# Two mixture-of-experts layers: experts sorted by their tokens, packed into 128-row sets in strips of 32

## The reference

```python
scores = sigmoid(h @ w_router)                       # n_tok x 64
_, idx = top_k(scores + e_bias, 8)                   # 8 experts for each token
wts = take(scores, idx); wts = wts / wts.sum() * 2.5
for e in range(64):                                  # rows of h that chose e
    a = silu(xb @ w_gate[e]) * (xb @ w_up[e])        # 1024 -> 256
    y = a @ w_down[e]                                # 256 -> 1024
out[token] += weight * y                             # plus one shared expert
```

## Time and profile before

| | us |
|---|---|
| median of 3 runs | 3415.65 (3410.34 to 3419.3) |
| the profiled execution | 3413.98, its span 3412.2 |
| PE busy in the span | 3240.7 (95%) |
| DVE, ACT, POOL busy | 2408.5, 1136.2, 418.6 |
| experts of layer 0 | from 1929.57 to about 2564 |
| experts of layer 1 | from about 2886.6 to 3384 |

### The profile page before, as it was taken

One profiled execution on the slowest core, in us unless ns is written; L12 is line 12 of the kernel. 1 busy time (PEld: TensorE's weight loads), 2 busy tenths in 40 slices (PEclk: granted clock), 3 DMA queues, 4 the chain that ended last, 5 costly groups with the idle time before them and its releaser, 6 DMA issues.

```text
span 3412.2 us, 53247 instructions
## 1 busy us (share of the span) xinstructions
PE 3240.7 (95%) x21848; PEld 2603.4 (76%) x21848; DVE 2408.5 (71%) x2973; ACT 1136.2 (33%) x1729; POOL 418.6 (12%) x308
## 2 busy tenths in 40 slices
PE   8998899999998799999889999999998989999997
PEld 8997688999997589999655677777777767455554
DVE  8887777887887778787666888888876564423223
ACT  1013232200004323211233488888873143111112
POOL 0101100010100200011000144434420010000000
PEclk9998999999999899999999999999999999999998
DMA  6555434445455434454102599999977215999994
GB/s 247 186 190 196 151 112 148 173 177 185 182 184 202 163 115 151 180 185 162 50 25 99 202 377 380 374 369 369 372 300 289 98 63 236 419 421 421 421 421 176
DMA packets 102708, 782.53 MB, mean 229 GB/s; under 512 B 19632, under 2 KB 21680, under 8 KB 31920
## 3 DMA queue, kind: packets, MB, share of 16 engines
q1 hardware_dynamic: 80064, 736.19, 56.0%
q0 software_dynamic: 20304, 41.72, 3.3%
q10 hardware_dynamic: 2080, 1.05, 0.1%
HBM read 776.26 MB, written 37.22 MB: 238 GB/s over the span
## 4 chain that ended last, share of the span: by engine, by line
PE 79%; DVE 14%; ACT 3%; issue 1%; DMA 1%; DVEq 0%; SPq 0%; POOL 0%; ACTq 0%; POOLq 0%
PE ps L457 76%; PE ps L476 3%; DVE ring_r L404 2%; DVE ring_r L403 1%; DVE ring_r L422 1%; DMA ring<-yd_dram 1%; DVE ring L1395 1%; DVE arena L2343 1%; DVE arena L1268 1%; DVE arena L1246 0%; ACT arena L1508 0%; ACT ring_r L416 0%; DVE arena L1225 0%; DVE arena L1253 0%; ACT ring L1508 0%
## 5 line engine op out<-in xcount | busy, mean ns | idle before, releaser
L457 PE MATMUL ps<-arena_r,ring_r 128*128 128x256 f32 (+1 forms) x9776 | 1279.3, 289 | 36.0 <-DVE ring_r L404 15.7
L457 PEld LDWEIGHTS ps<-arena_r,ring_r 128*128 128x128 f32 x9776 | 1218.4, 190 | 72.4 <-DVE ring_r L404 15.9
L457 PE MATMUL ps<-ring,arena 128*64 128x512 f32 (+3 forms) x2220 | 499.6, 537 | 4.5 <-DVE arena L1268 2.9
L457 PE MATMUL ps<-ring_r,arena_r 128*128 128x512 f32 (+1 forms) x1754 | 465.1, 386 | 1.3 <-DVE arena_r L2212 0.9
L404 DVE TENSOR_TENSOR ring_r<-ring,ring_r 128x4096 fp32r<-128x4096 f32 (+2 forms) x104 | 445.4, 4283 | 3.6
L457 PEld LDWEIGHTS ps<-ring,arena 128*64 128x64 f32 (+2 forms) x2220 | 178.8, 144 | 261.5 <-issue 240.3
L457 PEld LDWEIGHTS ps<-ring_r,arena_r 128*128 128x128 f32 x1754 | 312.3, 188 | 66.1 <-DVE arena_r L2212 1.3
L403 DVE CAST ring_r<-ring 128x4096 fp32r<-128x4096 f32 (+2 forms) x104 | 256.3, 2464 | 55.8 <-PE ps L457 44.1
L457 PE MATMUL ps<-arena_hi,arena_r 128*128 128x512 f32 x772 | 254.3, 397 | 2.3 <-DVE ring_r L2948 2.3
L457 PE MATMUL ps<-arena 64*128 64x128 f32 (+5 forms) x1408 | 199.3, 324 | 48.4 <-DVE ring L1395 16.1
L457 PEld LDWEIGHTS ps<-arena 128*128 128x128 f32 (+1 forms) x1408 | 151.8, 203 | 92.4 <-ACT arena L1809 33.8
(11 more groups left out here) (409 smaller groups left out, 3715.0 us busy)
## 6 DMA issues: line engine op xcount, KB each, us to landing
ring<-wexp_dram SPq DMA_DIRECT2D x396, 1024.0 KB, 9.5
ring<-stream_dram SPq DMA_DIRECT2D x143, 2048.0 KB, 7.7
ring<-yd_dram SPq DMA_DIRECT2D x4, 2048.0 KB, 11.3
arena<-yd_dram SPq DMA_DIRECT2D x2, 2048.0 KB, 10.3
consts_sb<-consts_dram SPq DMA_DIRECT2D x1, 2242.0 KB, 16.1
arena<-mem_dram POOLq DMA_DIRECT2D x2, 1024.0 KB, 7.1
xd_dram<-arena POOLq DMA_DIRECT2D x4, 512.0 KB, 9.8
arena<-yd_dram SPq DMA_DIRECT2D x4, 512.0 KB, 6.5
```

Source lines behind the costliest of these rows:

```text
L457: return pe.e.matmul(ps, lhsT=lhsT, rhs=rhs, start=start, stop=stop, skip_group_check=True)
```

## The change

Both layers get one class, `Sets`, in place of `Section` and `Pairs`.

- **Places.** The 64 experts of a layer are put on 64 places with a fixed capacity in strips of 32 rows (`CAPS`): 176 strips in layer 0, 104 in layer 1. The first four places hold experts 0 to 3; the others are filled in the order of their token counts. The order is found on the chip: `dve_keys` makes a key of count and number, `dve_beats` compares all with all, a matmul with ones (`pe_order`) counts the wins, a second one (`pe_firsts`) spreads each expert's first row and capacity.
- **Sets.** Four strips make a set of 128 rows: 44 sets in layer 0 for 65 blocks, 26 in layer 1 for 33.5 pairs. An expert can lie across two sets. In each step of k, `pe_hidden` and `pe_down` run over the pieces of the set with one instruction for each tile that `strips` cuts: 128, 64 or 32 stationary columns. By the layout, layer 0 has 10 sets of one piece of 128 columns, 10 of 64+64, 11 of 64+32+32 and 13 of 32+32+64; layer 1 has 10 of 64+64 and 16 of 64+32+32.
- **Arithmetic.** Layer 0 is plain fp32 throughout; the splits of rows and weights on ACT, DVE and PE go.
- **Weights.** Each of 64 experts is loaded once a layer (before: 65 and 67). The expert of a place above the fourth is read from a register. Layer 0 has 14 slots in place of 8, layer 1 has 10 as before. In layer 1 `down(i)` follows `hidden(i)` at once, not one set later.
- **One-hots of layer 1** are made piece by piece (one `tensor_scalar` for each piece and 128 tokens, twice), and the ranks and weights are put in the order of the places by PE ("turned", "is at", "by place").
- **Surplus.** Tokens past a place's capacity go to guarded sections of 128-row blocks.

```diff
-SLOTS = {0: 128, 1: 64}
-SECTIONS = {0: ((0, 65), (65, 68), (68, 96)), 1: ((0, 67), (67, 71), (71, 96))}
+SECTIONS = {0: ((0, 64), (64, 68), (68, 116)), 1: ((0, 64), (64, 68), (68, 96))}
 NBLK = 96
-NRAW = 8
-NPAIR = 10
+NRAW = {0: 14, 1: 10}
+FIXED = 4
+CAPS = {0: [3, 3, 3, 3] + [3, 2, 3, 4, 2, 2] * 8 + [5, 3, 3, 2, 3, 2, 2, 5, 3, 3, 2, 3],
+        1: [2, 2, 2, 2] + [2, 1, 1, 3, 1] * 4 + [2, 1, 1, 2, 2] * 8}
+SETS = {l: sum(CAPS[l]) // 4 for l in CAPS}
...
+def plan_places(l):
+
+    caps = CAPS[l]
+    assert len(caps) == 64 and sum(caps) % 4 == 0 and (l == 0 or max(caps) < 4 and sum(caps[:FIXED]) == 8)
+    falling = sorted(range(FIXED, 64), key=lambda p: -caps[p])
+    ranks = list(range(FIXED)) + [0] * (64 - FIXED)
+    for r, p in enumerate(falling):
+        ranks[p] = FIXED + r
+    firsts, sets, at_ = [], [[] for _ in range(sum(caps) // 4)], 0
+    for p, c in enumerate(caps):
+        firsts.append(32 * at_)
+        done = 0
+        while done < c:
+            s, o = divmod(at_ + done, 4)
+            n = min(c - done, 4 - o)
+            sets[s].append((p, 32 * done, o, n))
+            done += n
+        at_ += c
+    return ranks, firsts, [32 * c for c in caps], sets
...
+def strips(pieces):
+
+    for p, first, o, n in pieces:
+        while n:
+            m = 4 if n == 4 else 2 if n >= 2 and o % 2 == 0 else 1
+            yield p, o, m
+            o, n = o + m, n - m
...
+        def pe_order(pe, l):
+            ps = take(pe, "order", l)
+            pe.wait_ge(*at("beaten", l))
+            mm(pe, ps[:, 0:64], con("one1")[0:64, :], BEATS[0:64, :], True, True).then_inc(*pe.mark("ps", "order", l))
+
+        def pe_firsts(pe, l):
+            ps = take(pe, "firsts", l)
+            pe.wait_ge(*at("placed", l))
+            mm(pe, ps[:, 0:128], con("one1")[0:64, :], PLACED[0:64, :], True, True).then_inc(*pe.mark("ps", "firsts", l))
+
+        def pe_experts_of(pe, l, name):
+            ps = take(pe, name + " of", l)
+            pe.wait_ge(*at(name, l))
+            tr(pe, ps[0:1, 0:128], bef).then_inc(*pe.mark("ps", name + " of", l))
...
+        def dve_keys(dve, l):
+
+            counts = bank("counts", l)[:, 0:64]
+            dve.wait_ge(*at("ps", "counts", l))
+            dve.next.scalar_tensor_tensor(KEY, counts, 64.0, KEY_ADD, ALU.mult, ALU.add).then_inc(*dve.mark())
+            dve.next.tensor_copy(CNT, counts).then_inc(*dve.mark("left", "counts", l))
+
+        def dve_beats(dve, l):
+            dve.next.tensor_tensor(BEATS[0:64, :], KEY[0:64, :], ident[0:64, 0:64], ALU.mult).then_inc(*dve.mark())
+            dve.next.tensor_reduce(KEY_OF[0:64, :], BEATS[0:64, :], AX.X, ALU.add).then_inc(*dve.mark())
+            dve.next.tensor_scalar(BEATS[0:64, :], KEY[0:64, :], KEY_OF[0:64, :], None, ALU.is_lt).then_inc(*dve.mark("beaten", l))
...
+        class Sets:
 
 
             def __init__(self, l, b0, b1):
-                self.l, self.b0, self.n, self.key = l, b0, b1 - b0, (l, b0)
-                self.split = True
-                (self.pe, self.dve, self.act, self.pool), self.weights, self.x, self.y = SEC[l, b0]
+                self.l, self.b0, self.key = l, b0, (l, b0)
+                self.sets = PLACES[l][3] if b0 == 0 else [[(b, 0, 0, 4)] for b in range(b0, b1)]
+                self.s0 = 0 if b0 == 0 else SETS[l] + b0 - 64
+                self.n = len(self.sets)
+                self.done, self.weights, self.x, self.y = SEC[l, b0]
+                self.slots = len(self.weights)
...
                 for i in range(self.n + 1):
                     if i < self.n:
-                        self.items += [("a", i), ("b", i)]
-                    if i:
-                        self.items.append(("d", i - 1))
-                self.place = {it: j for j, it in enumerate(self.items)}
-                self.hi_at = [rings_r[:, 2048 * (NRAW + i):2048 * (NRAW + i) + 2048] for i in range(10 - NRAW)] + [h[:, :] for h in hi_parts[:2 if self.split else 3]]
-                self.down_at = [hi_parts[2][:, 0:1024], hi_parts[2][:, 1024:2048]]
-
-            def order(self):
+                        self.items += [(part, p) for part in "ab" for p in new[i]]
+                    if i and l == 0:
+                        self.items += [("d", p) for p in new[i - 1]]
+                    if i < self.n and l == 1:
+                        self.items += [("d", p) for p in new[i]]
+                self.place = {it: i for i, it in enumerate(self.items)}
...
+            def homes(self):
+
                 c0 = first_shared[self.l]
                 s = [2 * ((c0 + d) % NSLOT) + j for d in (2, 0, 1) for j in (0, 1)]
-                return s[0:2] + [6, 7] + s[2:]
-
-            def raw(self, part, i, of=rings):
-                o = 2048 * self.order()[self.place[part, i] % NRAW]
+                ring_of = [(rings, 2048 * j) for j in s]
+                hi_of = [(rings, 2048 * j) for j in (6, 7, 8, 9)]
+                if self.l:
+                    return ring_of[0:2] + hi_of + ring_of[2:]
+                here = [(arena, HT.base + 2048 * j) for j in (0, 1)] + hi_of[2:] + ring_of[2:] + [(arena, Ur.base + 2048 * j) for j in (0, 1)]
+                return ring_of[0:2] + hi_of[0:2] + here
+
+            def free(self):
+
+                l, c0 = self.l, first_shared[self.l]
+                if l:
+                    return [at("released", c0 - 1)] * 6 + [at("released", c0)] * 2 + [at("shared", l)] * 2
+                return [at("released", c0 - 1)] * 4 + [at("rows", l)] * 2 + [at("ps", "list", l, 3)] * 2 + [at("released", c0)] * 2 + [at("shared", l)] * 4
...
+        def pe_hidden(pe, S, i, ps, rows, *ready):
+
+            for k in range(KT):
+                part = "a" if k < 4 else "b"
+                for p, o, m in strips(S.sets[i]):
+                    pe.wait_ge(*at(*ready, k // (KT // 2) if S.l == 0 else k // 2))
+                    pe.wait_ge(*S.got(part, p))
+                    ins = mm(pe, ps[32 * o:32 * o + 32 * m, :], rows(k, 32 * o, 32 * m), S.raw(part, p)[:, col(k % 4, 512)], k == 0, k == KT - 1)
+                    if k % 4 == 3:
+                        ins.then_inc(*pe.mark())
+                if k % 4 == 3:
+                    for p in S.ends(i):
+                        pe.here(S.key, "used", part, p)
+            pe.here("ps", S.key, "hidden", i)
...
+        def pe_down(pe, S, i, turned):
+
+            for nn in range(2):
+                ps = take(pe, S.key, "y", i, nn)
+                for k in range(2):
+                    for p, o, m in strips(S.sets[i]):
+                        w = 1024 * k + 512 * nn
+                        pe.wait_ge(*at("left", S.key, "h", i))
+                        pe.wait_ge(*S.got("d", p))
+                        ins = mm(pe, ps[32 * o:32 * o + 32 * m, :], turned.v(128 * k + 32 * o, 32 * m), S.raw("d", p)[:, w:w + 512], k == 0, k == 1)
+                        if k == 1:
+                            ins.then_inc(*pe.mark())
...
-                xl, xh = as_r(XTb[i % 2].v()), as_r(XH[i % 2].v())
-                for k in range(KT):
-                    part = "a" if k < 4 else "b"
-                    wh, wl = S.hi(part, i)[:, col(k % 4, 512)], S.raw(part, i, rings_r)[:, col(k % 4, 512)]
-                    pe.wait_ge(*at("left", K, "x", i, k // 4))
-                    pe.wait_ge(*at(K, "split", part, i))
-                    mm(pe, ps[:, :], xh[:, col(k)], wh, k == 0, False)
-                    mm(pe, ps[:, :], xh[:, col(k)], wl, False, False)
-                    ins = mm(pe, ps[:, :], xl[:, col(k)], wh, False, k == KT - 1)
-                    if k % 4 == 3:
-                        ins.then_inc(*pe.mark(K, "used", part, i))
...
-        def dve_low_half(dve, S, part, i):
-            dve.wait_ge(*at(S.key, "high", part, i))
-            dve.next.tensor_tensor(S.raw(part, i, rings_r), S.raw(part, i), S.hi(part, i).bitcast(F32),
-                                   ALU.subtract).then_inc(*dve.mark(S.key, "split", part, i))
...
+                if p >= FIXED:
+                    eng.wait_ge(*at("left", "surplus of" if p >= 64 and l else "experts of", l))
+                e = slice(p, p + 1)
+                if p >= FIXED:
+                    e = bass.ds(sp.value_load(ber[0:1, p:p + 1], min_val=0, max_val=63), 1)
...
+                for p, counted, o, w in pieces():
+                    rank = RANK[tk].v(p, 1) if early else PRANK[tk].v(p, 1)
+                    free()
+                    dve.next.tensor_scalar(onehot(OHG, g, tk, o, w, True), counted, rank, None, ALU.is_equal).then_inc(*dve.mark(K, "onehot", g))
```

More of the change, by code:

```diff
@@ L199, in make_consts @@
     put("eps", np.full((128, 1), 1e-6))
+    for l in range(2):
+        for name, of in zip(("rank", "first", "cap"), PLACES[l]):
+            put(f"{name}{l}", np.concatenate([of, np.full(64, -1)])[:, None])
     put("hones", (i[:, None] // 64 == i[None, :] // 64))
@@ L2821, in got_x, with got @@
+            def got(self, part, p):
+                i = self.place[part, p]
```

(47 more changed lines are left out.)

799 lines of the change are left out of this document (316 added, 483 removed).

## The result

The changed kernel takes 3715.8 us (median of 4 runs, 3712.6 to 3719.4) against 3417.5 (4 runs) on the same chip: a ratio of 1.088, 95% interval 1.087 to 1.090. It is 298 us slower. The forecast was 3735, the range 3290 to 3790.

A forecast was written before the change was run, and what follows sets the result against it. PE was taken to pace layer 0 alone, with PE and DMA both at their limit in layer 1. 3414.0 + 209 (layer 0) + 111 (layer 1) - 1 (routing and entry) = 3733, about 3735 us; range 3290 to 3790.

The forecast's parts named there:

- The bound: Expert layers before the change: PE alone paces layer 0; in layer 1 PE and DMA are both at their limit.
- The step on which all turned: Mixed sets, both layers: each step of k is two visits of 1.02 us, 24.4 us a set.
- Layer 0: Expert stretch of layer 0: 20 one-width sets and 24 mixed sets take 842 us against 633, +209.
- Layer 1: Expert stretch of layer 1: 10 sets of 64+64 and 16 mixed sets take 609 us against 498, +111.
- Routing and entry: Routing +4 in layer 0 and +3 in layer 1, splits gone at layer 0's entry -8: together -1 us.
- The cover: Both expert layers: weight loads and row transfers hide beneath PE, with the DMA share falling to 0.65 to 0.8.
- Sum: Whole kernel: 3414.0 + 209 + 111 - 1 = 3733, about 3735 us.
- The first: Mixed sets: unequal widths on disjoint columns overlap, so DMA paces; 3320 us in all, chance 0.26.
- the fuller ring: Start of layer 0, if unequal widths overlap and DMA paces: more weight slots filled, -10 us.
- The second: Mixed sets: widths run one after another without a toll, 20.6 us a set; 3584 us in all, chance 0.06.
- The third: Expert layers: counts exceed the places and a guarded section runs, some 60 us more; 3795 on the forecast, chance 0.03.
- the fourth: Layer 1: DMA paces and PE's waits lower its clock, 0.86 us a record; about 3570 us in all, chance 0.01.

The follow-up runs named there:

- the run with one width: Changed kernel with every piece of a mixed-width set cut into 32-column tiles: 3319.4 us, 0.972 of the kernel before.
- width by width: Changed kernel with tiles still mixed, but all steps of k of one width before those of the other: 3623.6 us, 1.062 of the kernel before.

## Why the prediction was right, step by step

- **The bound.** That PE paces layer 0 alone and layer 1 with DMA close behind held, and so did its consequence: once PE is out of the way, layer 1 stops at 192 x 2.46 = 472 us, and ran in 472.
- **The step on which all turned.** Two visits a step of k for 64 and 32 columns; they do not overlap. I had it at 0.62 from rows in which a change of width only held back the next weights. The alternating loads and the run with one width show it, and the one width by width the toll. The rows pointed that way and did not prove it; what was right before the runs was the mechanism, at that chance. The visit was mis-sized by a little: 0.99 us, not 1.02, because I gave it the whole 0.16 us that a block needs for entering and leaving; the toll between 64 and 32 columns is 0.13 to 0.14. A mixed set is 23.8 us, not 24.4.
- **Layer 0**, forecast +209: measured +205. 24 x (23.82 + 1.39) = 605, 10 sets of 128 at 11.40 (10.31 and transposes of 0.87 and 0.22) and 10 of 64+64 at 11.99 make 839 by the chain's pieces, 838 in the trace.
- **Layer 1**, forecast +111: measured +97.5. This is the term most off. The mixed set's period is 28.28 and not 28.8 (16 sets, 8 us), and the stretch before was 500.9 and not 498 (3 us); the first and last sets lack some of their neighbours' gather and combine.
- **Routing and entry**, forecast -1: measured +4.3 for layer 1's (+3 forecast), -0.4 for the entry (+4 and -8, so -4). The entry's -0.4 came out near its forecast by luck. The first choice of experts on DVE starts at 1848.76 us before and at 1844.38 after, in code that the change leaves alone; among the profiled executions of all ten kernels it starts between 1841.0 and 1857.6. From there to the first `hidden` it is 80.8 us before and 84.8 after: +4.0 where -4 was forecast. The term mis-sized is the two round trips to PE (order, firsts). They were put at 1 us each, with no row behind it, and make 6.8 of the 8 us by which this stretch was missed; DVE stands still for them 6.08 and 2.75 us (timeline of DVE, after), as in PE's order two steps of k of the shared expert stand before the one (3.73 us) and three before the other (3.12):

```profile
1865.96 0.70 DVE L2763 TENSOR_SCALAR arena<-ps,consts_sb 64x64 f32<-64x64 f32 x2 [6.08 <-PE ps L490]
1869.42 0.29 DVE L2775 COPY arena<-ps 128x128 f32<-128x128 f32 x1 [2.75 <-PE ps L490]
```

  Behind the last set, 4.7 us went that I had not counted.
- **The cover.** Loads and row transfers lay beneath PE, at a share of 0.71 and 0.74 in the windows shown (forecast 0.65 to 0.8). The 14 slots were worth nothing in the changed kernel.
- **Sum.** 3412.2 (the span) + 205 + 97.5 + 4.3 - 0.4 - 4.7 = 3713.9, the span after 3713.3. The forecast was 19 above the median, 13.5 of them in layer 1.
- **The rivals.** The first was priced at layer 0 575 us (565 with the 10 that it gave the fuller ring), layer 1 472 and 3320 in all; the kernel in which tiles do overlap has 564, 472 and 3319. The second, without a toll, came to 20.6 us a mixed set; width by width shows 21.4 with six tolls, the changed kernel 23.8 with 24. The third did not occur (384 loads), nor the fourth (clock 1.00 in both stretches). Three of the prediction's sums are off, none so that it matters: by its terms the second rival's layer 1 is 549 and not 551, the fourth's total about 3590 and not 3570 (3319, and 744 for 472 in layer 1), and a toll of 0.05 us a visit would give about 3630, below its own range's 3650.

On the two pages of the Trainium skill that disagreed: "TensorEngine Tiling (Array Packing)", section Tiling Modes, lets a change of tiling mode drain TensorE, and these traces agree, at 0.13 to 0.17 us a change beside the overlap. "TensorE: Matmul & The Clock Gate", Part 3, with tiles of different column groups running side by side, holds for four tiles of 32 and two of 64 here (10.57 and 10.60 us a set) and not for 64 with 32 (23.8 us, 0.99 between their loads); the measurement decides.

## What to carry to other kernels

Give all column tiles that are meant to run side by side one width, the narrowest that any piece needs; a step with two widths is two steps. The runs show this for plain fp32 with 128 rows and 512 moving columns; other shapes and types were not run. More instructions of 32 columns cost TensorE little: 10.57 against 10.31 us in `hidden` and `down` of a set, and with the transposes 11.96 against 11.40, all of it about what four changes of width cost. Where one resource hides another, look at what the second will pace once the first is repaired: here DMA, at 2.46 us for each MB of weights, stands under both expert layers, and only there do a larger ring (9 us) and fewer loads begin to count.

The change with one width in a set, one more condition in `strips`, beats both kernels: 3319 us, 0.972 (0.970 to 0.975) of before and, by the two ratios to before, 0.893 (0.890 to 0.897) of the change as made.

## What was not expected

- The toll depends little on the widths: 0.16 to 0.17 us between 128 and 32 columns, 0.13 to 0.14 between 64 and 32. The transposes pay it too: eight of them take 0.87 us beside a set of 128 columns and 1.02 beside narrower tiles.
- Two bounds within 3% of each other (459 and 472 us) gave not the larger but 479: the larger has to be taken in each stretch of a layer, not once for the whole.
- With DMA pacing at a share of 1.01, TensorE's waits stay under 3 us each, and its granted clock in the windows shown is 0.97 and 1.00 (0.96 over all of layer 1): the fourth rival, a clock at half, would not have come even then.
